# Attention on one core: the small VectorE operations made once per two heads, and a third pair of score buffers

## The reference

```python
# "window": banded attention with context keys and a sink, 512 keys per query
p = softmax(concatenate([s_win, s_ctx, sinks]))      # the sink adds one column
o = p[..., :kw] @ vb + p[..., kw:kw + C] @ vc
# "ab": 16 causal heads with a position bias, one softmax per head
# "nsa": compressed + selected + window attention, three softmaxes per head, mixed by gates
e = exp(s - max(s)); p = e / sum(e)
```

## Time and profile before

| | us |
|---|---|
| median of 3 runs | 2639.03 (2637.43 to 2646.86) |
| the profiled execution, its own time | 2641.11 |
| its span, first to last instruction | 2639.0 |
| PE busy | 2524.8 (96%) |
| DVE busy | 1361.3 (52%) |
| ACT busy | 1156.6 (44%) |
| mean granted clock of TensorE | 0.969 of full speed |

### The profile page before, as it was taken

One profiled execution on the slowest core, in us unless ns is written; L12 is line 12 of the kernel. 1 busy time (PEld: TensorE's weight loads), 2 busy tenths in 40 slices (PEclk: granted clock), 3 DMA queues, 4 the chain that ended last, 5 costly groups with the idle time before them and its releaser, 6 DMA issues.

```text
span 2639.0 us, 40053 instructions
## 1 busy us (share of the span) xinstructions
PE 2524.8 (96%) x15799; PEld 2157.9 (82%) x15799; DVE 1361.3 (52%) x2130; ACT 1156.6 (44%) x1827; POOL 23.7 (1%) x37
## 2 busy tenths in 40 slices
PE   7999999998999999999999998999989998989998
PEld 4777787875777778777788767999869998868998
DVE  4322334895523333423233577555777665786665
ACT  3333323474433322333322356554556555566554
POOL 0000000000000000000000000000000001000000
PEclk8999999999999999999999899999989998989999
DMA  7444542200344432344423211544414555413553
GB/s 314 161 159 179 189 160 93 96 33 1 143 159 173 176 130 110 112 177 173 159 96 112 98 63 67 187 177 175 179 65 175 182 186 191 157 41 125 178 191 144
DMA packets 52725, 374.88 MB, mean 142 GB/s; under 512 B 5822, under 2 KB 7034, under 8 KB 8736
## 3 DMA queue, kind: packets, MB, share of 16 engines
q1 hardware_dynamic: 50000, 358.63, 37.1%
q0 software_dynamic: 2208, 14.37, 1.6%
q10 hardware_dynamic: 432, 0.73, 0.1%
HBM read 372.55 MB, written 7.39 MB: 144 GB/s over the span
## 4 chain that ended last, share of the span: by engine, by line
PE 89%; DVE 6%; ACT 2%; issue 1%; DMA 1%; SPq 0%; ACTq 0%; DVEq 0%
PE acc L1845 27%; PE acc L1846 26%; PE acc L1847 26%; PE bank L1922 3%; DVE sc L1746 1%; PE bank L1949 1%; DMA ada_raw<-in_slabs 1%; DVE wlo L1299 1%; DVE sc L1775 1%; ACT sc L1192 1%; PE acc L2316 1%; DVE prod L591 1%; PE bank L1980 1%; PE acc L2342 1%; DVE prod L1663 0%
## 5 line engine op out<-in xcount | busy, mean ns | idle before, releaser
L1299 DVE TENSOR_TENSOR wlo<-raw,whi 128x1024 fp32r<-128x1024 f32 x534 | 646.9, 1223 | 902.1 <-ACT whi L767 901.6
L767 ACT ACTIVATE whi<-raw 128x1024 fp32r<-128x1024 f32 x534 | 556.0, 1055 | 972.2 <-PE acc L1847 924.4
L1845 PE MATMUL acc<-hhi,whi 128*128 128x256 f32 (+1 forms) x2808 | 950.6, 339 | 27.4 <-DVE hlo L1381 10.5
L1846 PE MATMUL acc<-hlo,whi 128*128 128x256 f32 (+1 forms) x2808 | 936.9, 334 | 0.0
L1847 PE MATMUL acc<-hhi,wlo 128*128 128x256 f32 (+1 forms) x2808 | 936.5, 334 | 0.0
L1845 PEld LDWEIGHTS acc<-hhi,whi 128*128 128x128 f32 x2808 | 539.9, 192 | 111.3 <-issue 58.5
L1846 PEld LDWEIGHTS acc<-hlo,whi 128*128 128x128 f32 x2808 | 540.5, 192 | 50.1 <-issue 1.7
L1847 PEld LDWEIGHTS acc<-hhi,wlo 128*128 128x128 f32 x2808 | 539.9, 192 | 50.7
L1845 PE MATMUL acc<-ghi,whi 128*128 128x512 f32 (+1 forms) x1056 | 357.1, 338 | 0.0
L1847 PE MATMUL acc<-ghi,wlo 128*128 128x512 f32 (+1 forms) x1056 | 357.0, 338 | 0.0
L1846 PE MATMUL acc<-glo,whi 128*128 128x512 f32 (+1 forms) x1056 | 357.0, 338 | 0.0
(11 more groups left out here) (269 smaller groups left out, 2251.1 us busy)
## 6 DMA issues: line engine op xcount, KB each, us to landing
raw<-in_slabs SPq DMA_DIRECT2D x329, 1024.0 KB, 4.8
ada_raw<-in_slabs SPq DMA_DIRECT2D x10, 1024.0 KB, 25.5
skew_dram<-lines_dram POOLq DMA_DIRECT2D x1, 6144.0 KB, 23.6
bt<-skew_dram POOLq DMA_DIRECT2D x4, 1024.0 KB, 9.5
x<-in_x_in SPq DMA_DIRECT2D x1, 2048.0 KB, 18.0
mlp<-in_slabs POOLq DMA_DIRECT2D x2, 1024.0 KB, 6.2
out<-x SPq DMA_DIRECT2D x1, 1024.0 KB, 4.8
rope<-in_rope POOLq DMA_DIRECT2D x1, 512.0 KB, 4.0
```

The costliest lines, as they stand in the source:

```text
L767: nc.scalar.activation(whi[:, n % 2, cols], raw_of(n, cols), ACT.Copy).then_inc(ready, 1)
L1299: nc.vector.tensor_tensor(wlo[:, n % 2, cols], raw_of(n, cols), whi[:, n % 2, cols].bitcast(F32), ALU.subtract).then_inc(low, 1)
L1845: nc.tensor.matmul(out, w[0], xx[0], start=first, stop=False)
L1846: nc.tensor.matmul(out, w[0], xx[1], start=False, stop=False)
```

## The change

- The one-column operations of DVE (the exp's bias from the maximum, the sink's addition, the reciprocal, the gates) are made for a pair at once, on tiles of 2 x 1 or 2 x 2 numbers per row, and signal once per pair. The sink enters through a table of negated sinks, made once at the start. Additions with maxima and row scalings stay one by one.
- Six score buffers take the place of four. The two new ones lie in storage that the stage doesn't use otherwise (`Vm`, or part of `QK` in "nsa").
- Scores, maxima and exps run one pair further ahead: iteration `u` makes `scores(u+6)`, `biased` of `u+6` and `u+7`, and `exps` of `u+6` and `u+7`. Ahead of the loop stand six units of each. `exps` now waits until both units of its pair have their maxima, and `normalised` until both have their exps.

```diff
+        neg_sink = sb("neg_sink", [P, NH])
-            stt4 = sb("stt4", [P, 4, 10], F32, at)
+            stt6 = sb("stt6", [P, 6, 10], F32, at)
+        def probs(st, u):
+            more = QK[:, 12:16, :].rearrange("p (a b) t -> p a (b t)", a=2) if st.what == "nsa" else \
+                Vm[:, :, :].rearrange("p (a b) t -> p a (b t)", a=2)
+            return sc[:, u % 6, :] if u % 6 < 4 else more[:, u % 6 - 4, :]
-            pool.sem_inc(t_ready, 4)
+            pool.sem_inc(t_ready, 6)
...
                 def exps(u):
-                    act.wait_ge(m_ready, A0 + u + 1)
+                    act.wait_ge(m_ready, A0 // 2 + u // 2 + 1)
...
+                exps(4)
+                exps(5)
                 for u in range(0, UNITS, 2):
...
-                    if u + 4 < UNITS:
-                        exps(u + 4)
-                        exps(u + 5)
+                    if u + 6 < UNITS:
+                        exps(u + 6)
+                        exps(u + 7)
...
+                s = VCOL["sink"]
+                step.done(nc.vector.tensor_scalar(neg_sink[:, :], vec[:, s:s + NH], -1.0, None, ALU.mult))
...
                 def biased(u):
+                    q, b, h = rows_of(u), u % 6, head_of(u)
                     keys = 512 if win else P * (q + 1)
+                    for v in (u, u + 1):
+                        dve.wait_ge(s_ready, A0 + v + 1)
+                        dve.wait_ge(t_ready, A0 + v + 1)
+                        bias = mask[:, q, :] if win else bt[:, head_of(v), P * (1 - q):S]
+                        for s in range(2 if nsa else 1):
+                            ins = nc.vector.tensor_tensor_reduce(probs(st, v)[:, keys * s:keys * s + keys],
+                                                                 B[v % 4][:, keys * s:keys * s + keys], bias,
+                                                                 1.0, LOWEST, ALU.add, ALU.max,
+                                                                 stt6[:, v % 6, s:s + 1])
+                        ins.then_inc(s_free, 1)
+                    dve.wait_ge(s_free, 4 + A0 + u + 2)
+                    w = 2 if nsa else 1
+                    top, low = stt6[:, b:b + 2, 0:w], stt6[:, b:b + 2, 2:2 + w]
                     if win:
+                        sinks = neg_sink[:, h:h + 2].rearrange("p (a b) -> p a b", b=1)
+                        ins = nc.vector.scalar_tensor_tensor(low, top, -1.0, sinks, ALU.mult, ALU.min)
                     else:
+                        ins = nc.vector.tensor_scalar(low, top, -1.0, None, ALU.mult)
                     ins.then_inc(m_ready, 1)
                 def normalised(u):
+                    sums2, parts = stt6[:, b:b + 2, 4:4 + w], stt6[:, b:b + 2, 7:7 + w]
+                    dve.wait_ge(e_ready, A0 + u + 2)
                     if win:
+                        step.done(nc.vector.tensor_tensor(sums2, sums2, stt6[:, b:b + 2, 6:7], ALU.add))
+                    step.done(nc.vector.reciprocal(parts, sums2))
                     if nsa:
+                        two = gates[:, q, 3 * h:3 * h + 6].rearrange("p (a b) -> p a b", b=3)
+                        step.done(nc.vector.tensor_tensor(parts, parts, two[:, :, 1:3], ALU.mult))
+                    for v in (u, u + 1):
+                        for s in range(w):
+                            p = probs(st, v)[:, keys * s:keys * s + keys]
+                            ins = nc.vector.tensor_scalar(p, p, stt6[:, v % 6, 7 + s:8 + s], None, ALU.mult)
+                        ins.then_inc(p_ready, 1)
...
-                for u in range(4):
-                    biased(u)
+                biased(0)
+                biased(2)
+                biased(4)
                 normalised(0)
-                normalised(1)
                 for u in range(0, UNITS, 2):
                     if u + 2 < UNITS:
                         normalised(u + 2)
-                        normalised(u + 3)
-                    if u + 4 < UNITS:
-                        biased(u + 4)
-                        biased(u + 5)
+                    if u + 6 < UNITS:
+                        biased(u + 6)
...
+                scores(4)
                 for u in range(0, UNITS, 2):
-                    if u + 4 < UNITS:
-                        scores(u + 4)
+                    if u + 6 < UNITS:
+                        scores(u + 6)
```

More of the change, by code:

```diff
@@ L1186, in exps @@
                 def exps(u):
[L1188 to L1189 removed]
+                    act.wait_ge(m_ready, A0 // 2 + u // 2 + 1)
+                    sp = stt6[:, u % 6]
                     keys = 512 if st.what == "window" else P * (rows_of(u) + 1)
                     for s in range(2 if st.what == "nsa" else 1):
[L1192 to L1193 removed]
+                        ins = nc.scalar.activation(probs(st, u)[:, keys * s:keys * (s + 1)],
+                                                   probs(st, u)[:, keys * s:keys * (s + 1)], ACT.Exp,
                                                    bias=sp[:, 2 + s:3 + s], accum_out=sp[:, 4 + s:5 + s])
@@ L1737, in biased @@
                 def biased(u):
-                    q, b = rows_of(u), u % 4
-                    sp = stt4[:, b]
+                    q, b, h = rows_of(u), u % 6, head_of(u)
                     keys = 512 if win else P * (q + 1)
-                    dve.wait_ge(s_ready, A0 + u + 1)
-                    dve.wait_ge(t_ready, A0 + u + 1)
-                    bias = mask[:, q, :] if win else bt[:, head_of(u), P * (1 - q):S]
-                    for s in range(2 if nsa else 1):
-                        ins = nc.vector.tensor_tensor_reduce(sc[:, b, keys * s:keys * s + keys],
-                                                             B[u % 4][:, keys * s:keys * s + keys], bias,
-                                                             1.0, LOWEST, ALU.add, ALU.max, sp[:, s:s + 1])
@@ L1751, in biased @@
+                    dve.wait_ge(s_free, 4 + A0 + u + 2)
+                    w = 2 if nsa else 1
+                    top, low = stt6[:, b:b + 2, 0:w], stt6[:, b:b + 2, 2:2 + w]
                     if win:
-                        sink = VCOL["sink"] + head_of(u)
-                        ins = nc.vector.tensor_scalar(sp[:, 2:3], sp[:, 0:1], vec[:, sink:sink + 1], -1.0,
-                                                      ALU.max, ALU.mult)
-                    else:
-                        w = 2 if nsa else 1
-                        ins = nc.vector.tensor_scalar(sp[:, 2:2 + w], sp[:, 0:w], -1.0, None, ALU.mult)
+                        sinks = neg_sink[:, h:h + 2].rearrange("p (a b) -> p a b", b=1)
+                        ins = nc.vector.scalar_tensor_tensor(low, top, -1.0, sinks, ALU.mult, ALU.min)
+                    else:
+                        ins = nc.vector.tensor_scalar(low, top, -1.0, None, ALU.mult)
@@ L1759, in biased @@
                     ins.then_inc(m_ready, 1)
                 def normalised(u):
-                    q, b = rows_of(u), u % 4
-                    sp = stt4[:, b]
-                    dve.wait_ge(e_ready, A0 + u + 1)
+                    q, b, h = rows_of(u), u % 6, head_of(u)
+                    w = 2 if nsa else 1
+                    sums2, parts = stt6[:, b:b + 2, 4:4 + w], stt6[:, b:b + 2, 7:7 + w]
+                    dve.wait_ge(e_ready, A0 + u + 2)
                     if win:
-                        step.done(nc.vector.tensor_tensor(sp[:, 4:5], sp[:, 4:5], sp[:, 6:7], ALU.add))
@@ L1767, in normalised @@
-                    w = 2 if nsa else 1
-                    step.done(nc.vector.reciprocal(sp[:, 7:7 + w], sp[:, 4:4 + w]))
+                        step.done(nc.vector.tensor_tensor(sums2, sums2, stt6[:, b:b + 2, 6:7], ALU.add))
+                    step.done(nc.vector.reciprocal(parts, sums2))
                     if nsa:
-                        g = 3 * head_of(u) + 1
-                        step.done(nc.vector.tensor_tensor(sp[:, 7:9], sp[:, 7:9], gates[:, q, g:g + 2], ALU.mult))
+                        two = gates[:, q, 3 * h:3 * h + 6].rearrange("p (a b) -> p a b", b=3)
+                        step.done(nc.vector.tensor_tensor(parts, parts, two[:, :, 1:3], ALU.mult))
@@ L1772, in normalised @@
                     keys = 512 if win else P * (q + 1)
-                    for s in range(w):
-                        p = sc[:, b, keys * s:keys * s + keys]
-                        ins = nc.vector.tensor_scalar(p, p, sp[:, 7 + s:8 + s], None, ALU.mult)
-                    ins.then_inc(p_ready, 1)
+                    for v in (u, u + 1):
[3 more added lines that the diff above has]
+                        ins.then_inc(p_ready, 1)
```

9 lines of the change are left out of this document (2 added, 7 removed).

## The result

| | before | after |
|---|---|---|
| median | 2639.4 us (5 runs, 2637.4 to 2646.9) | 2625.0 us (5 runs, 2620.5 to 2626.7) |
| ratio | | 0.9927, 95% interval 0.9915 to 0.9940 |
| profiled execution, span | 2639.0 us | 2621.3 us |
| window, ab, nsa | 65.4, 62.9, 68.4 us | 59.0, 59.9, 70.2 us |
| all outside the three stages | 2442.3 us | 2432.2 us |

By the ratio the gain is some 19 us, by the medians 14.

The account below looks back on a forecast made before the run. DVE was taken to pace the window stage at 3.70 us a pair. Gains of 7.2 + 2.7 + 6.0 = 15.9 us, taken as 15, led from 2641.11 to 2626.1, a forecast median of 2624, range 2616 to 2636.

Parts of the forecast that it names:

- What bounds the window stage: Window: DVE sets the pace at 3.70 us a pair, PE alone could do 3.11; the stage gains 7.2 us.
- the one-column operations: DVE in the three stages: joining them saves 0.65 us a pair in window and nsa, 0.45 in ab, 28.0 in all.
- The 0.4 that I put as an upper bound: DVE: most that one combined small operation could take, in us; 0.2 was assumed.
- One pair further ahead: Attention stages: lookahead ends DVE's 0.21 us wait for an exp; the four-engine loop then takes 3.14 us a pair in window.
- slow rival: Attention loop: handoffs 0.3 us slower each, at ACT's wait for both maxima, make the kernel 5 us slower, 2644; chance 0.08.
- Nsa, -6.0: Nsa stage: 4.7 us from two pairs in 6.50 instead of 7.28, 1.4 at the end, less 0.1.
- Ab, -2.7: Ab stage: DVE savings give 2.9 us, the end 1.2, and a later `turned(0)` costs 1.4.
- The rest, nothing: Outside the stage schedules: negated sinks and moved buffers cost nothing, place at most 0.01 us each way per operation.
- The clock's rival: Stages: shorter PE waits save four half-clock stretches, 6 us more, total 2618; chance 0.13.
- The sum: Three stages: 7.2 + 2.7 + 6.0 = 15.9 us gained, taken as 15.
- What I said would show it: Trace: small operations halved, window PE iteration 3.1 to 3.2 us, nsa two 6.5, stages 58, 60, 62, `turned(0)` 1.4 later.

Follow-up runs that it names:

- e2_noshift: Changed kernel with the negated sinks' table moved behind `stt6`, so buffers ahead lie as in the kernel before; 2634.4 us, ratio 0.9962 to the kernel before.
- e5_pairs: Changed kernel with small operations still per pair, but four score buffers and scores, maxima and exps at `u+4`; 2652.0 us, ratio 1.0040 to the kernel before.
- e3_outlo: Changed kernel with DVE's `out_lo` moved behind `biased(u+6)`, to the end of the iteration; ratio 0.9927 to the kernel before, nsa 68.4 us.
- e4_nsa: Changed kernel with `out_lo` behind `biased(u+6)` and, in nsa, ACT's `PcT` copy ahead of the exps; ratio 0.9927 to the kernel before, nsa 64.3 us.
- E10_mid: e9_both with DVE's `out_lo` between `normalised(u+2)` and `biased(u+6)`; 2588.5 us, ratio 0.9796 to the kernel before.
- e7_place: e4_nsa with `hhi`, `hlo`, `ghi`, `glo`, `ohi`, `olo` at 176 and `whi`, `wlo` at 64 past a multiple of 256 B; 2597.1 us, ratio 0.9825.
- e9_both: e4_nsa with `ghi`, `glo` at 128 past a multiple of 256 B, and h and g on columns 48 to 303 for 256 tokens; 2590.9 us, ratio 0.9803.
- e1_shift: Kernel before plus one unused 64 B per partition buffer behind `two_gains`; 2633.95 us beside 2643.1, ratio 0.9964.
- e8_before_both: Kernel before with the placing of e9_both and the old attention schedule; 2608.4 us, ratio 0.9867.
- m2_map: Separate kernel timing matmuls over 256 address pairs of moving and stationary operand in the kernel's strides; 24 pairs under 119 ns, the rest up to 123.6.
- m1_offsets: Separate kernel timing 256-column matmuls with either operand moved in 16 B steps, alone and beside other engines and transfers; moving offsets gave 114.7 to 121.4 ns.

## Why the prediction was right, and where it was wrong

*What bounds the window stage, and the one-column operations*: right. A combined operation costs 0.16 to 0.17 us (I took 0.2), and most pairs pass in 3.1 to 3.3 us, three of them in 3.6 to 4.2; window gave 6.4 us for 7.2. About 1.2 of the 6.4 is clock: e2_noshift has the same schedule and took 60.2 at 0.97, where the changed kernel took 59.0 at 1.00. The busy time of DVE in the stages fell by 23.7 us (28.0 forecast), 0.18 for each of the 128 operations. The 0.4 that I put as an upper bound needed no guess: the trace before has the gates of nsa (line 1771) on two columns, at 162 ns.

*One pair further ahead*: the step is right for the whole change and wrong as a reading of it. I took the lookahead as the end of a 0.21 us wait and booked the gain to the saved operations. e5_pairs shows that these, alone, cost about 0.8% (2652.0 us), since the joined waits close a loop of 4.65 us between DVE and ACT. My slow rival had the right place (ACT's wait for both maxima) and a wrong price: 0.3 us a handoff, while what the join costs is the work of the other engine. The lookahead hid it. The rule of the Trainium skill that I set beside that rival ("Perfetto Trace Analysis", section "Optimizing Scalar/DVE Operations": where ScalarE and VectorE aren't saturated but cause bubbles on other engines, breaking up instructions may let work complete sooner) agrees with e5_pairs, where DVE and ACT wait 24.1 and 23.1 us for each other in a stage of 78.

*Nsa, -6.0*: wrong, +1.8. I went through the loop of scores, exps, copies and values, and left out two other rows of ACT's queue. First, the `PcT` copy: it stands behind the exps of iteration 0, and these became two of 256 keys for each unit where they were of 128. PE's wait for it went from 1.2 to 4.20 us, and the first values start 12.0 us into the stage for 10.4 before, where I had taken off 0.1 for the start; with the copy ahead of the exps they start at 8.9, and that is worth 4 us (e3_outlo to e4_nsa). The half clock is no part of this miss: 14.9 us of it in the changed kernel, 13.7 before. Second, `out_hi`, for which `out_lo` waits at the head of DVE's iteration; I counted `out_lo` as 0.17 a pair and no wait. E10_mid takes that wait away, and by the estimate there it is worth about 1 us. With both repaired nsa takes 62.6 us, the 62 that I forecast, but with 8.1 us less at half clock than in the changed kernel, some 2.5 us by the same estimate; without that luck it would be near 65.

*Ab, -2.7*: it came as -3.0, but that isn't shown to be the schedule. `turned(0)` starts 8.48 us after the stage's start, 7.23 before, so the cost of 1.25 is as forecast (1.4, though the terms that I listed for it add up to 1.16). But the granted clock went from 0.93 to 1.00, and up to (1.00 - 0.93) x 62.86 = 4.4 us hang on that. E2_noshift, with the same ab code, took 59.9 (clock 1.00). With `out_lo` at the end of the iteration it was 60.1 (e3_outlo, 1.00), 65.2 (e4_nsa, 0.87), 63.7 (e7_place, 0.91) and 64.0 us (e9_both, 0.89). The old schedule took 64.0 (e1_shift, 0.95) and 64.2 us (e8_before_both, 0.87). At 0.95 to 0.96 the new one is ahead (60.8 in e10_mid, which moves more than this, against 64.0), at 0.87 it is behind (65.2 against 64.2). What the schedule gives in ab stays open.

*The rest, nothing*: this failed. I wrote "at most 0.01 each way per operation" for the place of buffers and stopped there. The measured effect, 0.0053 us, lies inside that bound, but 15,799 matmuls stand behind it: multiplied out, the bound was 158 us each way and should have been in the sum as an open term. The evidence I gave was of DVE on two PSUM banks, and the effect is TensorE's on SBUF.

*The clock's rival*: it came in part. In the three stages 26.0 us at half clock became 14.9, all of it gained in window and ab, and at 0.31 us each some 3.4 of the measured 7.6 us are this (an estimate, with the price of nsa). It doesn't follow from the change alone: e4_nsa had 27.6 again.

*The sum*: 15.9 forecast in the stages, 7.6 measured there, and 10.1 elsewhere. The total was met by luck, by two errors of opposite sign: nsa 7.8 too good, placing 10.1 left out.

*What I said would show it*: the counts, the PE iteration in window, window's length within 1 us and `turned(0)` were met. Two pairs in nsa took 6.75 to 7.02 us in the steady part, not 6.5. "DVE waits for transposes rather than for exps" was not: it waits for `out_hi`.

## What to carry to other kernels

Joining small operations of two units is worth its time on the engine, but it joins their waits as well: work out the loop in which each engine waits for both units, and add a stage of lookahead with the join, not after it. When a step of one engine moves ahead, list everything that stands behind it in that engine's queue, the rare items too (here a copy made twice and one made every other iteration). And when a diff allocates a buffer, count what is allocated behind it: a bound per operation means nothing until it is multiplied by the number of operations.

## What the runs showed of the hardware

- The pitch of float32r matmuls (the time from one start to the next) depends on the pair of SBUF addresses of moving and stationary operand modulo 256 B. At full clock the stages that hold one value have 113.3 or 120.0 ns with 256 columns, 226.7 or 233.3 with 512 (others lie between), 6.67 ns apart, which is 16 cycles at the 2.4 GHz level. About one pair in ten is fast with 256 columns, and a pair that is fast with one width need not be so with the other: with both operands at 128 past a multiple of 256 B it is 120.0 and 226.7.
- The addresses aren't all of it. At one placing the same stretches ran at 113.3 ns in e9_both and, for some 200 us behind an attention stage, at 117.8 in e10_mid. By the table of m2_map, (128, 0) with 512 columns held 232.4 in two stages and 233.3 in the third of one execution. (48, 192) has 227 with 512 columns in m2_map but 231.1 in e7_place. None of these is explained.
- With 256 columns it is no contention: with ACT and DVE busy for 97% of the time and 419 GB/s arriving the values of m1_offsets repeat to 0.1 ns.
- Shifts of 64 B by one unused buffer made a kernel of 2643 us 9 us faster; placing for both widths made it 36 us faster (e8_before_both). Two versions can therefore differ by some 1% for a reason that their instructions don't show, and a comparison should hold the addresses still, as e2_noshift does.
- The same ab code behind the same wait of 2.01 us went at a granted clock of 1.00 in one execution (e3_outlo, 60.1 us) and 0.87 in another (e4_nsa, 65.2 us). Differences of a few us between single profiles of a stage with waits in it aren't differences of the schedule.
